# Second FFN of a decoder trunk: the weight sums of the second halved pair before the low parts of g, and a half lot's split at another place

## The reference, cut to what matters

```python
def swiglu(x, w1, w3, w2):
    return (jax.nn.silu(x @ w1) * (x @ w3)) @ w2
...
    x = x + 0.5 * swiglu(rms_norm(x, ffn2_norm[l]), ffn2_w1[l], ffn2_w3[l], ffn2_w2[l])
```

## Time and profile before

| | us |
|---|---|
| median of 3 runs | 2779.62 (2779.6 to 2779.7) |
| profiled execution | 2779.76 |
| its span, first to last instruction | 2777.7 |
| TensorE busy | 2769.2 |
| VectorE busy | 1753.7 |
| ScalarE busy | 1277.0 |
| GpSimd busy | 853.2 |

### The profile page before, as it was taken

The page is one execution under the profiler, slowest core; times in us unless marked ns, Lnnn a source line. Parts: engine busy times, 40 slices in busy tenths (PEclk is TensorE's granted clock), DMA queues, the critical chain, the costliest instruction groups (busy, mean ns, idle before and its releaser), DMA issues.

```text
span 2777.7 us, 41457 instructions
## 1 busy us (share of the span) xinstructions
PE 2769.2 (100%) x15682; PEld 2334.4 (84%) x15682; DVE 1753.7 (63%) x2756; ACT 1277.0 (46%) x1956; POOL 853.2 (31%) x416
## 2 busy tenths in 40 slices
PE   9999999999999999999999999999999999999999
PEld 8888888877788889898988888888777888898988
DVE  5585557685657448585744855576856674585755
ACT  5343344556355446353543423445553553463533
POOL 0075014333333343131100850233333343431321
DMA  5323584222222222232333235732222222223322
GB/s 199 98 91 118 141 152 122 83 74 71 80 88 77 91 94 98 92 114 99 107 129 98 91 129 136 159 107 82 71 76 76 84 84 91 94 90 104 109 95 103
DMA packets 113092, 284.57 MB, mean 102 GB/s; under 512 B 35616, under 2 KB 45344, under 8 KB 112416
## 3 DMA queue, kind: packets, MB, share of 16 engines
q1 hardware_dynamic: 112928, 282.35, 33.2%
HBM read 268.67 MB, written 9.44 MB: 100 GB/s over the span
## 4 chain that ended last, share of the span: by engine, by line
PE 96%; DVE 1%; DMA 1%; SPq 0%; ACT 0%; issue 0%; POOL 0%; DVEq 0%; ACTq 0%
PE bank L594 24%; PE bank L596 24%; PE bank L595 24%; PE bank L678 5%; PE bank L679 5%; PE bank L680 5%; PE bank L622 1%; PE bank L624 1%; PE bank L623 1%; PE bank L988 1%; PE bank L1007 1%; PE bank L1022 1%; PE bank L768 1%; PE bank L1121 1%; PE bank L962 0%; DMA s_ud<-s_uc 0%
## 5 line engine op out<-in xcount | busy, mean ns | idle before, releaser
L464 POOL TENSOR_TENSOR w_lo<-raw,w_hi 128x1024 fp32r<-128x1024 f32 x208 | 519.6, 2503 | 1081.5 <-ACT w_hi L456 1081.5
L594 PE MATMUL bank<-h_hi,w_hi 128*128 128x512 f32 x1840 | 724.1, 394 | 0.4 <-DVE silu_a L2177 0.3
L596 PE MATMUL bank<-h_hi,w_lo 128*128 128x512 f32 x1840 | 716.6, 389 | 0.0
L595 PE MATMUL bank<-h_lo,w_hi 128*128 128x512 f32 x1840 | 716.4, 389 | 0.0
L456 ACT ACTIVATE w_hi<-raw 128x1024 fp32r<-128x1024 f32 x374 | 393.4, 1056 | 565.7 <-PE bank L596 537.5
L594 PEld LDWEIGHTS bank<-h_hi,w_hi 128*128 128x128 f32 x1840 | 345.4, 188 | 78.3 <-issue 7.1
L596 PEld LDWEIGHTS bank<-h_hi,w_lo 128*128 128x128 f32 x1840 | 345.3, 188 | 72.9
L595 PEld LDWEIGHTS bank<-h_lo,w_hi 128*128 128x128 f32 x1840 | 345.6, 188 | 69.5
L464 DVE TENSOR_TENSOR w_lo<-raw,w_hi 128x1024 fp32r<-128x1024 f32 x166 | 230.8, 1390 | 169.9 <-ACT w_hi L456 169.6
L514 POOL TENSOR_TENSOR w_lo<-raw,w_hi 128x1024 fp32r<-128x1024 f32 x80 | 146.6, 1853 | 438.0 <-DVE bank L2228 403.3
L594 PE MATMUL bank<-g_hi,w_hi 128*128 128x512 f32 x698 | 272.1, 390 | 0.2
(11 more groups left out here) (441 smaller groups left out, 5243.0 us busy)
## 6 DMA issues: line engine op xcount, KB each, us to landing
raw<-in_w_lots SPq DMA_DIRECT2D x478, 512.0 KB, 3.5
s_wd<-s_z SPq DMA_DIRECT2D x8, 512.0 KB, 3.8
s_t<-s_taps SPq DMA_DIRECT2D x16, 256.0 KB, 14.0
da_s<-da_qk SPq DMA_DIRECT2D x16, 256.0 KB, 3.8
x<-in_x SPq DMA_DIRECT2D x8, 256.0 KB, 5.9
raw_k<-in_w_lots SPq DMA_DIRECT2D x8, 256.0 KB, 6.1
s_w_re<-s_wd SPq DMA_DIRECT2D x32, 64.0 KB, 3.5
s_w_im<-s_wd SPq DMA_DIRECT2D x32, 64.0 KB, 3.5
```

What stands on the lines that cost most here:

```text
L464: eng.tensor_tensor(w_lo[:, s], raw[:, s], w_hi[:, s].bitcast(f32), SUB).then_inc(S["lo_done"], 1)
L594: pe.matmul(b[:, :], w_hi[:, s, kw], xh[:, k], start=(k == 0), stop=False)
L595: pe.matmul(b[:, :], w_hi[:, s, kw], xl[:, k], start=False, stop=False)
L596: return pe.matmul(b[:, :], w_lo[:, s, kw], xh[:, k], start=False, stop=(k == nk - 1))
```

## The change

Three edits, each acting in both layers (GpSimd's clear of the semaphores and its wait for `g_done` stay as they are):
- VectorE makes T1 of pair 1 directly behind `whole(n + 2, 1)`, then `multiply(1)`, then T3, then `take_y` of pair 0 and the rest of pair 1's sums and low parts. The two low parts of g stand behind all of these, and a wait for the first of them is added.
- ScalarE makes the high half of n+5 ahead of the norm's logarithm.
- GpSimd starts the low half of n+5 on the sum S4 of h, where it waited for the first product g (`gated_done`).

```diff
--- before.py
+++ after.py
@@ -1464,7 +1464,7 @@
                         pool.wait_ge(S["x7_in_t_sum"], t_at(n, T3))
                         low_of(pool, n)
                         if HALVED[n] == 0:
-                            pool.wait_ge(S["gated_done"], G(1) + 1)
+                            pool.wait_ge(S["x7_in_t_sum"], s_at(S4))
                         low_of(pool, n + 1, 4)
                         if layer < DEPTH - 1 and HALVED[n] == 0:
 
@@ -1611,13 +1611,13 @@
                         high(act, n + 4)
                         round_t(n + 4, T2)
                         round_t(n + 4, T4)
+                        high(act, n + 5, 4)
                         log = log_of(2)
                         round_s(S1)
                         rstd_of(2, log)
                         for j in (S3, S2, S4):
                             round_s(j)
                         silu(n, 0, g0)
-                        high(act, n + 5, 4)
                         high(act, n + 6)
                         round_g(0, g0)
                         copy_x(n + 4)
@@ -2326,18 +2326,19 @@
                         lows_of_h()
                         multiply(0, g0)
                         whole(n + 2, 1)
-                        low_g(0, g0)
+                        add_t(n + 6, T1)
                         multiply(1, g0)
-                        add_t(n + 6, T1)
+                        add_t(n + 6, T3)
                         take_y(n + 4, 2)
-                        low_g(1, g0)
-                        add_t(n + 6, T3)
                         low_t(n + 6, T1)
                         add_t(n + 6, T2)
                         low_t(n + 6, T3)
                         low_t(n + 6, T2)
                         add_t(n + 6, T4)
                         low_t(n + 6, T4)
+                        low_g(0, g0)
+                        low_g(1, g0)
+                        V.wait_ge(S["g_done"], g0 + 1)
                     for i in range(i0 + (th == 0), J):
                         a = n + 2 * i
                         more = i + 1 < J
```

## The result

The changed kernel takes 2786.27 us (median of 11 runs, 2786.07 to 2787.67), the kernel before 2779.70 in the same session (11 runs): 6.57 us more, a ratio of 1.0024 with a 95% interval of 1.0015 to 1.0033. It is slower: the interval excludes no change, though the 0.24% is little more than the 0.2% that such a measurement can tell. The profiled execution took 2786.26 us with a span of 2784.2, 6.5 more than the span before.

What follows compares the result with a forecast made beforehand. TensorE, busy 2769.2 of 2777.7 us, was taken to bound the kernel. Added to the median 2779.62, 4.73 (clear), 0.0 (layer 1) and 1.7 (clock), 6.4 us together, gave 2786.0 us, range 2783.7 to 2787.6.

Steps and rivals of the forecast that it cites:

- The clear holds lot n+6: Layer 0, GpSimd: the clear waits for low_g(0) and delays the lot; TensorE's 1.40 us stall becomes 6.13, losing 4.73 us.
- The wait moves to q7 in layer 1: Layer 1, pair 1: q1's 1.40 us stall goes, TensorE waits about 1.4 us for VectorE's take_y instead; net 0.0 us.
- The clock: TensorE after layer 0's long stall: 18 passes at 1.2 GHz instead of 2.4, 1.7 us lost; could be 0.5 to 3.
- The sum: Whole kernel: 4.73 + 0.0 + 1.7 = 6.4 us added to the median 2779.62, giving 2786.0 us.
- The cover in layer 0: Layer 0, pair 1: take_y near 1088.5 to 1089, q7 at 1090.94, covered by 1.5 us or more, so q7 does not wait.
- The n+5 piece: Half lot moved earlier on ScalarE and GpSimd: nought; 0.5 us if ScalarE's cover failed, s_lo 0 to 0.1 us.
- (b): Rival: clear held and wait moved as forecast, but TensorE's clock holds after the stall; 4.7 us, 2784.3; chance 0.26.
- (c): Rival: layer 1 gain stands, take_y of pair 1 sooner; 1.5 us less, 2782.8 with clock held, 2784.5 without; chance 0.06.
- (d): Rival: not slower, GpSimd's clear does not hold lot n+6 in layer 0; 2776.6 to 2779.6; chance 0.05.
- (e): Rival: VectorE in layer 0 falls behind beyond its cover, q7 or q6 of pair 1 waits 1 to 2 us more; 2787 to 2788; chance 0.08.

Runs made afterwards that it cites:

- the busy gap: Changed kernel plus 50 extra TensorE passes of 256 columns ahead of q1 of pair 1 in layer 0, result unused: 2784.19 us.
- the two last experiments: Changed kernel, clear behind pair 1's lots, low_g(1) behind take_y of pair 1: 2778.86 us; the same with low_g(0) moved to GpSimd: 2777.58 us.
- The stalls of chosen length: Kernel before, GpSimd recomputing parts of lot n+6 ahead of the real one to delay it, in three kernels: 2786.53, 2793.39 and 2784.25 us.
- the kernel with stalls of up to 1.93 us: Changed kernel with low_g(0) on VectorE directly behind take_y of pair 0, GpSimd's clear left where it is: 2782.21 us.

## Why the prediction was right, step by step

- **The clear holds lot n+6.** Forecast 1079.14 for the clear and a wait of 6.13 us; 1078.5 and 6.22 measured, with this execution 0.57 ahead. The term was 4.73 us, measured 6.22 - 1.40 = 4.82 by the waits and 4.5 by the median of the kernel with the busy gap. Shown by moving the clear alone, and by VectorE's order alone.
- **The wait moves to q7 in layer 1.** Forecast about 1.4 us and a net of 0.0; measured 1.38 us ahead of q7 and none at q1. The reading behind it, that VectorE needs 6.04 us from take_v to take_y whatever TensorE does, is borne out by the rows (6.04 us from 2469.70 to 2475.74) and by the two last experiments: one slot off the list takes 0.5 us off the wait, two slots nearly all of it.
- **The clock.** Forecast 1.7 us from the program's start; measured: q1 and q3 of pair 1 last from 1081.74 to 1086.61, 4.87 us, where they took 24 x 0.12 = 2.9 and 0.1 for the first step, so 1.9 us. The busy gap gave 2.1. That the clock would fall stood at 0.55 against 0.26. The stalls of chosen length show it was far surer than that, and all eleven executions of the changed kernel show 0.999. That the price came so close is in part luck: the start of the program was the only row to take it from, and behind stalls of other lengths it was 1.3 to 2.5 us.
- **The sum.** 4.8 + 1.9 + 0.0 = 6.7 against a span longer by 6.5. The 0.2 left is made of the 0.57 us that this execution was ahead in front of layer 0's second FFN, and of some 0.4 us that it lost between there and layer 1's, which were not followed. Median 2786.27, forecast 2786.0.
- **The cover in layer 0.** take_y of pair 1 was put at 1088.5 to 1089; it started at 1090.35, 1090.9 on the scale of before, some 2 us later. What was missing is the slow passes, which the forecast left out of this path. ScalarE's copy_x of pair 1 waited for the last pass of q1 until 1084.71:

```profile
1084.71 0.37 ACT L1587 ACTIVATE bank<-bank 128x256 f32<-128x256 f32 x1 [6.58 <-PE bank L680]
```

  T1's rounding stood behind it, and VectorE's first low_t of pair 2 waited 1.35 us for that (1085.61). T1 of pair 2 was held by GpSimd too (1082.22, 1.44 us instead of 0.69), behind take_w (2.50 instead of 0.42), but that ended inside this wait and cost nothing. With the busy gap, where T1 was held just as long and no pass was slow, take_y of pair 1 started at 1088.64, 1089.0 on the scale of before, the upper end of the forecast. q7 came at 1092.33, 1.6 us behind take_y's end, because the same slow passes delayed it also. The verdict "covered" held.
- **The n+5 piece.** Forecast nought, measured nought; s_lo took 4.63 us for four, as before.

Of the rivals, (b), the one with the clock held (2784.3), is what the busy gap measured, 2784.2. (c), a gain that stands in layer 1, is refuted by the 1.38 us at q7. (d), in which the clear does not hold the lot, is refuted by the clear's start at 1078.5. (e), in which VectorE falls behind in layer 0 and TensorE waits for it, did not happen, though VectorE did fall behind by some 2 us: TensorE was late by as much.

## What to carry to other kernels

When a step is moved back on one engine, follow its semaphore through every list that waits for it, rare instructions included: here a clear that runs once held one lot and cost more than both stalls that the change aimed at could give. A wait taken from a saturated engine's early result reappears at its next late one, so shorten the list, not only its head. And price a stall of TensorE beyond its length: here each stall of 2.2 us or more cost another 1.3 to 2.5 us, and the kernel with stalls of up to 1.93 us very likely paid about 1.3 us in half of its executions.

## What the runs showed of the hardware

- Stalls of TensorE of 2.20, 2.48, 2.74, 3.82, 5.16, 6.19, 6.22 and 6.24 us were each followed or met by the lower clock, and those of up to 1.4 us were not. In the kernel with stalls of 1.54, 0.95 and 1.93 us the trace shows no fall, but five of its ten executions show a mean clock of 0.999 and took some 1.3 us longer. The lower level lasted 3.4 us with the four shorter and 6.8 to 6.9 us with the four longer ones, and with the four shorter it fell only when TensorE was at work again.
- The range clear of the semaphores takes 616 to 618 ns of GpSimd's queue; held until 1078.5, it kept the next lot until 1079.35, which started at 1073.38 with the clear out of the way.
- VectorE's operations with two SBUF operands were held by GpSimd's lots wherever they ran beside one for long: 2.48 us for 0.68, 2.50 for 0.42, 1.44 for 0.69. An overlap of 0.14 us left them as they were (s_lo at 1064.21, 4.63 us for four). Those with one operand in PSUM kept their length beside a lot.
